# Four adaLN slabs moved to layer 0's routing with the first gather held free, and a ninth place for layer 1's expert slabs

## What is computed

```python
sh1, sc1, g1, sh2, sc2, g2 = jnp.split(silu(c) @ w_ada[l] + b_ada[l], 6, axis=-1)   # and the same for c_ctx
h = modulate(rms_norm(x, norm1_g[l]), sh1, sc1)          # latent and context tokens
y = parallel_mixer(h, ...)     # neighbourhood attention and HGRN2 branches, sigmoid gates, w_out
x = x + g1 * y
h2 = modulate(rms_norm(x, norm2_g[l]), sh2, sc2)
x = x + g2 * grouped_moe(h2, w_router, ...)              # 16 experts, top 2 of the best group of 4
```

## Time and profile before

| what | us |
|---|---|
| median of 3 runs | 1500.55 |
| lowest and highest | 1500.09, 1509.64 |
| the profiled execution | 1510.84 |
| its span, first to last instruction | 1508.8 |
| mean granted TensorE clock in it | 0.968 of 2.4 GHz |

### The profile page before, as it was taken

How to read it: one execution, slowest core, us unless ns; L and a number is a source line. 1 busy time by engine, 2 the same in 40 slices (tenths; PEclk the granted TensorE clock), 3 DMA queues, 4 the chain that set the end, 5 groups by cost and what they waited for, 6 DMA issues and landing times.

```text
span 1508.8 us, 17997 instructions
## 1 busy us (share of the span) xinstructions
PE 1408.4 (93%) x7084; PEld 973.6 (65%) x7084; DVE 903.3 (60%) x1234; ACT 687.6 (46%) x962; POOL 202.3 (13%) x179
## 2 busy tenths in 40 slices
PE   3999999998999985999999969989998998999997
PEld 2786667645888854677777638876766996334333
DVE  3477986456744436988888824688586874222112
ACT  4553452246333345777777626543346453111002
POOL 0006970000000001211111020058000000000000
PEclk9999999999999987999999977999999998999999
DMA  9861104693131435999999975111444664999994
GB/s 356 238 175 58 38 19 168 246 388 147 56 112 57 182 112 199 366 388 401 401 400 400 345 272 213 56 57 56 167 157 179 258 245 168 381 429 428 426 428 165
DMA packets 96764, 352.19 MB, mean 233 GB/s; under 512 B 21792, under 2 KB 22944, under 8 KB 84128
## 3 DMA queue, kind: packets, MB, share of 16 engines
q1 hardware_dynamic: 93008, 337.95, 58.6%
q0 software_dynamic: 2976, 10.49, 2.1%
q10 hardware_dynamic: 688, 2.49, 0.4%
HBM read 341.48 MB, written 13.63 MB: 235 GB/s over the span
## 4 chain that ended last, share of the span: by engine, by line
PE 81%; DVE 6%; POOL 4%; ACT 3%; DMA 2%; issue 2%; another core or an unknown queue 1%; ACTq 0%; SPq 0%; DVEq 0%; POOLq 0%
PE bank L1412 7%; PE bank L832 4%; PE bank L1147 4%; PE bank L1144 4%; PE bank L1153 4%; PE bank L1434 4%; PE bank L724 3%; PE bank L970 3%; PE bank L972 3%; PE bank L975 3%; PE bank L743 3%; PE bank L680 2%; PE bank L1173 2%; PE bank L1178 2%; PE bank L1183 2%; PE bank L1445 2%
## 5 line engine op out<-in xcount | busy, mean ns | idle before, releaser
L2985 DVE TENSOR_TENSOR slab_lo<-slab,high 128x4096 fp32r<-128x4096 f32 x48 | 210.8, 4417 | 4.7 <-ACT high L2114 4.7
L2114 ACT ACTIVATE high<-slab 128x4096 fp32r<-128x4096 f32 x48 | 174.1, 3631 | 21.5 <-PE bank L1153 19.8
L2390 POOL DMA_INDIRECT feed_rows<-token_table,slot_token x16 | 45.1, 2820 | 549.8 <-DVE slot_token L2926 359.6
L1412 PE MATMUL bank<-narrow_slab,picked 128*64 128x512 f32 x256 | 113.2, 595 | 2.1 <-issue 1.7
L1413 PE MATMUL bank<-narrow_slab,picked 128*64 128x512 f32 x256 | 113.3, 595 | 0.0
L832 PE MATMUL bank<-hT,ring 128*128 128x512 f32 (+1 forms) x256 | 104.2, 545 | 0.0
L3150 DVE TENSOR_TENSOR hidden<-bank,gated 64x512 f32<-64x512 f32 x16 | 17.4, 1085 | 134.6 <-ACT gated L2269 134.6
L1412 PEld LDWEIGHTS bank<-narrow_slab,picked 128*64 128x64 f32 x256 | 33.7, 137 | 66.6 <-issue 65.2
L832 PEld LDWEIGHTS bank<-hT,ring 128*128 128x128 f32 x256 | 46.8, 194 | 33.2 <-issue 31.6
L1144 PE MATMUL bank<-high,feed_hi 128*96 128x512 f32 x256 | 66.8, 404 | 0.7 <-ACT feed_hi L2121 0.7
L1147 PE MATMUL bank<-high,feed_lo 128*96 128x512 f32 x256 | 64.9, 395 | 1.6 <-DVE feed_lo L2992 1.6
(11 more groups left out here) (415 smaller groups left out, 3154.3 us busy)
## 6 DMA issues: line engine op xcount, KB each, us to landing
ring<-in_w_in SPq DMA_DIRECT2D x23, 2048.0 KB, 12.5
ring<-in_w_ada SPq DMA_DIRECT2D x20, 2048.0 KB, 10.5
slab<-in_w_gate SPq DMA_DIRECT2D x16, 2048.0 KB, 12.9
slab<-in_w_up SPq DMA_DIRECT2D x16, 2048.0 KB, 13.9
slab<-in_w_down SPq DMA_DIRECT2D x16, 2048.0 KB, 14.4
narrow_slab<-in_w_gate SPq DMA_DIRECT2D x16, 2048.0 KB, 21.1
narrow_slab<-in_w_up SPq DMA_DIRECT2D x16, 2048.0 KB, 23.0
narrow_slab<-in_w_down SPq DMA_DIRECT2D x16, 2048.0 KB, 18.4
```

Source lines behind the costliest of these rows:

```text
L1412: T.matmul(bank[0][0:64, :], x, gate[:, k, :], start=(k == 0), stop=(k == KT - 1))
L2114: S.activation(half_of(e, kind)[:], w[:], ACT.Copy)\
L2985: V.tensor_tensor(low[:], w[:], half_of(e, kind)[:].bitcast(f32), ALU.subtract)\
```

## The change

Slabs 10 to 13 leave the attention of layer 0 and are done in the routing: slab 10 ahead of `place`, 11 behind it, 12 and 13 and the group's turn behind `slots`. The six slabs that stay beside the attention are at the even pairs 0 to 10. Slabs 10 and 13 are fetched into the slabs of up and down of expert 1, slabs 11 and 12 into the place of `high[0]` and `high[1]`. So the splits of expert 0 on ACT wait for slabs 11 and 12 to be done, and the fetches of up and down of expert 1 wait for slabs 10 and 13, and up also for the first gathered rows. DVE now starts its first split only when POOL has gone past its first gather (`slots_kept` at 2). In layer 1 a ninth place is at the address of `xT`; it is first filled when x has been copied into PSUM.

```diff
-    ADA_GROUPS = ((0, 2), (1, 3), (4, 5), (6, 7, 8, 9), (10, 11, 12, 13), (14, 15), ...
+    ADA_GROUPS = ((0, 2), (1, 3), (4, 5), (6, 7, 8, 9), (14, 15), (10, 11, 12, 13), ...
...
-    FIRST, AGAIN = (6, 7, 0, 1, 2, 3, 4, 5), tuple(range(LANES))
+    FIRST, AGAIN = (6, 7, 0, 1, 2, 3, 4, 5, 8), tuple(range(LANES))
...
-    narrow_at = slab_at[:SLOTS] + [B0, hT_at, A0 + 16 * KB, B0 + 16 * KB]
+    narrow_at = slab_at[:SLOTS] + [B0, hT_at, A0 + 16 * KB, B0 + 16 * KB, xT_at]
...
+    gap_slab = [fixed(f"gap_slab{i}", [P, SLOT], offset=A0 + (44 + 16 * i) * KB) for i in range(2)]
...
+        GAP_LANES = (6, 7, 6, 7)
...
-            loads += ada_loads[4:16] if l == 0 else ada_loads[20:24]
-            turn += [1, 2, 3, 1, 2, 0, 3, 1, 2, 0, 3, 1] if l == 0 else [1, 2, 3, 1]
+            loads += ada_loads[4:10] + ada_loads[14:16] if l == 0 else ada_loads[20:24]
+            turn += [1, 2, 3, 1, 2, 0, 3, 1] if l == 0 else [1, 2, 3, 1]
...
+            if l == 0:
+                loads += ada_loads[10:14]
+                lane += GAP_LANES
...
+        def ada_place(n):
+            gap = {10: slab[LANE[UP][1]], 11: gap_slab[0], 12: gap_slab[1], 13: slab[LANE[DOWN][1]]}
+            return front_slab[n][:] if n < len(front_slab) else gap[n][:] if n in gap else slot(ada_loads[n])
...
-                return 6 + p if 0 <= p < 10 else None
+                return {0: 6, 2: 7, 4: 8, 6: 9, 8: 14, 10: 15}.get(p)
...
# tensor engine, routing
+                if l == 0:
+                    ada_rows(10)
                 o = open_bank(("place", l), "place_ready")
...
                 if l == 1:
                     x_as_rows(0)
+                else:
+                    ada_rows(11)
...
                     mm.then_inc(sem["psum_ready"], 1)
+                    ada_rows(12)
+                    ada_rows(13)
+                    ada_turn(13)
...
# SP, the first slabs of layer 0's experts
+                    def fill_gap(n):
+                        there, count = full(ada_loads[n])
+                        if n >= 12:
+                            sp.wait_ge(there, count - 16)
+                        sp.dma_start(ada_place(n).rearrange("p (k n) -> p k n", k=KT), source(ada_loads[n])[0]).then_inc(there, 16)
...
+                        if (e, kind) == (1, UP):
+                            sp.wait_ge(*slot_spent[max(m for m in range(base) if lane[m] == i)])
+                            fill_gap(10)
+                            sp.wait_ge(*is_ready(("out", 0, KT - 1)))
+                            fill_gap(11)
+                            fill_gap(12)
+                            sp.wait_ge(sem["h_ready"], 2 * KT)
+                            fill_gap(13)
+                            sp.wait_ge(*slot_spent[slot_of(ada_loads[10])])
+                            sp.wait_ge(sem["rows_there0"], 16)
+                            fill_slab(e, kind)
+                            continue
+                        if (e, kind) == (1, DOWN):
+                            sp.wait_ge(*slot_spent[slot_of(ada_loads[13])])
+                            fill_slab(e, kind)
+                            continue
...
# SP, layer 1's experts
+                        elif at == FIRST[-1]:
+                            sp.wait_ge(sem["h_ready"], KT * 4)
+                            sp.wait_ge(*is_ready(("x_rows", 0)))
...
# scalar engine
+                    act.wait_ge(*slot_spent[slot_of(ada_loads[11])])
                     split_high(0, GATE)
+                    act.wait_ge(*slot_spent[slot_of(ada_loads[12])])
                     split_high(0, UP)
+                    ada_keep(13)
                     keep_feed(0)
...
# gpsimd, in the loop of gathers
+                    if e == 0:
+                        pool.sem_inc(sem["slots_kept"], 1)
...
# vector engine
+                    dve.wait_ge(sem["slots_kept"], 2)
                     split_low(0, GATE)
+                    ada_mod(13)
                     keep_feed(0)
                     split_low(0, UP)
+                    dve.wait_ge(sem["ada_mod"], ada_group(13)[0] + 1)
```

More of the change, by code:

```diff
@@ L82, in fixed @@
         return nc.alloc_sbuf_tensor_at(name, shape, dtype, offset=where)
+    xT_at = at[0]
     xT = fixed("xT", [P, KT, TOK])
@@ L94, in build @@
     router = fixed("router", [P, KT, 32])
-    ADA_GROUPS = ((0, 2), (1, 3), (4, 5), (6, 7, 8, 9), (10, 11, 12, 13), (14, 15), (16, 17, 18, 19), (20, 21, 22, 23))
+    ADA_GROUPS = ((0, 2), (1, 3), (4, 5), (6, 7, 8, 9), (14, 15), (10, 11, 12, 13), (16, 17, 18, 19), (20, 21, 22, 23))
     COND_AT = 6
@@ L376, in loads_before @@
             counts = [lane[:b].count(i) for i in range(len(FIRST))]
-            assert len(set(counts[:SLOTS])) == 1
+            assert ph == 3 or len(set(counts[:SLOTS])) == 1
             return counts
@@ L402, in result @@
             return bank[ready[key][0]]
+        skews = 4 * NA_HEADS * DEPTH
         scatter_bank = (1, 5, 6, 7, 1, 5, 6, 7)
@@ L666, in ada_rows @@
                 pe.wait_ge(*full(ada_loads[n]))
-                w = (front_slab[n][:] if n < len(front_slab) else slot(ada_loads[n])).rearrange("p (k n) -> p k n", k=KT)
+                w = ada_place(n).rearrange("p (k n) -> p k n", k=KT)
                 if first:
@@ L1057, in x_as_rows @@
                         for j in range(4):
-                            T.matmul(bank[b][:, j * P:(j + 1) * P], xT[:, 4 * half + j, SEG + t * P:SEG + (t + 1) * P],
-                                     ident, start=(j == 0), stop=False)
+                            mm = T.matmul(bank[b][:, j * P:(j + 1) * P], xT[:, 4 * half + j, SEG + t * P:SEG + (t + 1) * P],
+                                          ident, start=(j == 0), stop=False)
+                    jobs[0] += 1
+                    ready["x_rows", half] = (None, jobs[0], "psum_ready")
+                    mm.then_inc(sem["psum_ready"], 1)
                 if l == 1:
@@ L1596, in _ @@
                         sp.wait_ge(sem[f"tok_there{t}"], 32)
-                while n < base:
+                gap_loads = slot_of(ada_loads[10]) if l == 0 else base
+                while n < gap_loads:
                     if last_in(n) not in slot_spent:
@@ L1602, in _ @@
                         sp.wait_ge(*is_ready(("o", l, HG_HEADS - 1)))
[L1603 removed]
+                        sp.wait_ge(sem["bias_loaded"], 16 * (skews + l))
                         sp.dma_start(bias_skew[:].rearrange("p h q c -> p (h q c)"), skew_table[l]).then_inc(sem["bias_loaded"], 16)
@@ L1620, in _ @@
                     n += 1
-                if n < base or ("place", l) not in ready:
+                if n < gap_loads or ("place", l) not in ready:
                     break
@@ L2702, in window_bias @@
                     if h == 0:
-                        dve.wait_ge(sem["bias_loaded"], 16 * (l + 1))
+                        dve.wait_ge(sem["bias_loaded"], 16 * (skews + l + 1))
                     b = bias[:, h].rearrange("p q (r c) -> p (q r) c", c=GRID_W)
@@ L2845, in _ @@
                 wide_gates()
-                dve.wait_ge(sem["ada_mod"], ada_group(12 * l + 11)[0] + 1)
+                dve.wait_ge(sem["ada_mod"], ada_group(12 * l + (9, 11)[l])[0] + 1)
                 for d in range(KT * l):
```

5 lines of the change are left out of this document (2 added, 3 removed).

## The result

The changed kernel takes 1496.93 us (median of 20 runs, 1493.52 to 1502.56); the kernel before takes 1508.2 us (median of 20 runs, 1500.09 to 1511.44). The ratio is 0.9937 with an interval of 0.9926 to 0.9947: 0.63% faster, inside 1%. I had forecast 0.87% and 1487.5 us. Of the 9.4 us between 1487.5 and 1496.93 most is the base: the median of three runs from which I started, 1500.55, lay at the low end of what 20 runs show.

A forecast was written before the change was run, and what follows sets the result against it. PE, busy 93% of the span, was taken as the bound. Gains of 9.9 (attention), 1.5 (routing) and 1.75 us (ninth place) sum to 13.15, scaled to a median of 1487.5 us; range 1480 to 1498.

The forecast's parts named there:

- Part 1: Layer 0's attention: 11.9 us of slabs, turn and slab waits saved, less 2.0 of new DVE-chain waits: 9.9 us gained.
- some 1.8 us either way: Layer 0's attention: allowance for one half-clock stretch more or less as PE's stalls change.
- Part 2: Layer 0's routing: four slabs and a turn fit into PE's idle time and rows turn earlier: 1.5 us gained.
- DVE now stays off until POOL is past it: Routing, first gather: free of DVE's split it takes 0.92 us, so its rows could be turned 3.4 us earlier.
- fourth rival: Routing: POOL lets DVE go before the gather's descriptors are written; routing gains 0, 11.65 us in all, 1489.0; chance 0.14 or 0.07.
- Both share the DMA engines with the stores of the token rows: Routing: fetches of slabs 12 and 13 run beside the token stores at a DMA share of 0.52, cost 0.
- The third limit: Routing: ACT's late splits, adaLN row copy, turn and DVE's addition let `turn_rows` start at 584.0, not 585.65: 1.6 gained.
- Part 3: Layer 1's experts: slabs issued a place earlier remove PE's wait at expert 15: 1.75 us gained.
- the first: Rival, layer 0's attention: DVE's chain takes the slabs' place, only 4.5 us gained there; 1492.8 us in all; chance 0.13.
- The second: Rival, routing: the gap runs at half clock, a loss of 1.7 us there; 1490.7 us in all; chance 0.12.
- The third: Rival, routing: clock stays up, so `turn_rows` and expert 0's first eight matmuls save 2.1 us more; 1485.4; chance 0.14.
- The fifth: Rival, layer 0's experts: bound by fetches, pushed work costs about 15.6 us against 13.15 gained; 1503 us; chance 0.04.

The follow-up runs named there:

- run 5: The changed kernel itself measured once more, nothing altered: 1500.28 us, ratio 0.9949 to the kernel before.
- run 6: Changed kernel with adaLN slab 13's fetch cut to an eighth, its products reading slab 10's place: 1494.09 us, ratio 0.9908.
- run 7: Changed kernel without DVE's wait for `slots_kept` ahead of its first split: 1497.44 us, ratio 0.9936.
- run 12: The changed kernel itself measured a third time, nothing altered: 1502.42 us.
- run 3: Changed kernel with DVE doing its adaLN addition first, then waiting for the first gathered rows to land before its split: 1495.71 us, ratio 0.9921.
- run 2: Changed kernel with eight places for layer 1's slabs again in place of nine: 1499.27 us, ratio 0.9944.
- run 1: Changed kernel with slabs 10 to 13 left out wholly, with their fetches and waits, and without DVE's wait for `slots_kept`: 1496.95 us, ratio 0.9926.
- run 4: Changed kernel with the six attention slabs beside pairs 1, 2, 3, 7, 9 and 11 in place of the even pairs: 1488.03 us, ratio 0.9865.

## Why the prediction was right or wrong

**Part 1, the attention (9.9 us).** The mechanism was right. The waits came where the chain was drawn: 0.60 at pair 0 (I had said 0.5), 1.77 at pair 2 (1.7), 0.98 at pairs 6 and 10 (0.7); the 2.41 at pair 14 was there before, as 2.40. That is 2.5 us of new waits where I had 2.0, and no wait for a slab is left. In the profile the gain is 12.5, because the clock went from 0.95 to 1.00. With one stretch at half clock, as in runs 5, 6 and 7, it is 11.1; with three, as in run 12, it is 8.1. The attention before had two such stretches, one behind each of its two waits for the scaling (windows, the number ahead of the last two is the clock):

```profile
343.00:353.00 10.00, 8.46 (x50) 5.16 (x52) 7.64 (x23) 6.64 (x20) 0.00 (x0) 0.83 1.03 393
355.00:365.00 10.00, 6.82 (x42) 4.42 (x40) 4.40 (x13) 5.90 (x12) 0.00 (x0) 0.83 0.00 0
```

By the changed kernel's 59.5, 60.9 and 63.9 us with none, one and three, a stretch costs some 1.4 us; with two of them, as before, the gain would be 9.6 us by this estimate, and 9.9 was forecast. The term "some 1.8 us either way" for the clock was the mis-sized one: 59.5 to 63.9 us is what the same program shows. This is also part of why profile (16.3 us) and medians (11.3 us) differ: the profile of before was of one of its slowest executions (1510.84, the runs reach 1511.44), the one after of one of its fastest (1494.57, the runs begin at 1493.52).

**Part 2, the routing (1.5 us gained).** This is the step that failed. In the profile after it lost 1.5 us up to the first turn and 0.8 us more to the second (10.0 us from the first turn to the second, where it was 9.2), as more of expert 0's first products fell into half clock: 3.70 and 2.62 us for the first two groups of eight, before 3.40 and 2.03. Two sentences of it were wrong.

"DVE now stays off until POOL is past it, so it takes 0.92 and not 4.33 us": POOL's signal stands behind the gather in its program but comes ahead of its work: DVE had begun at 564.69, the gather at 564.88. That was my fourth rival, to which I gave 0.07. The first profile shows the gather caught in spite of the hold, and run 5 the same program with a gather that went through: the outcome is left to a race. Run 3 shows what a real hold would have been worth: 3.2 us of span. The rival had priced itself at no gain, and the measured loss of 1.5 is more: a caught gather ends 0.8 us behind the split, and the split now begins 7.3 us after `place` in place of 5.4, since ACT's split ahead of it waits for slab 11 (ACT begins at 560.62, 3.2 us after `place`; before it was 0.1 ahead of it).

"Both share the DMA engines with the stores of the token rows, but the share in 550 to 571 was 0.52. Cost 0": the window of that share ends at 571, where the last store is issued (570.55), and the stores land up to 576.3. It told nothing of what the stores meet. The window after, 539 to 557, in which all four are issued, is full:

```profile
539.00:557.00 18.00, 15.59 (x80) 6.98 (x78) 9.42 (x28) 14.18 (x28) 0.00 (x0) 0.81 1.05 389
```

The last store landed 8.9 us after its issue in place of 5.7, and the gather waits for it. Run 6 shows it by taking seven eighths of one fetch away. This error comes first: in the forecast the gather began 6.3 us after `place` (577.58) and the split 7.3 (578.6), so the gather would have gone through with no hold at all; in run 6 it began at 5.5 and did. It was the late stores that put it at 7.4, where only a hold that holds could have saved it.

The third limit, ACT's and DVE's chain behind the slabs, was right in kind and size: `place` to turn 12.4 us in run 3 and 13.3 in run 5 (its adaLN turn at half clock), against 14.4 before, 2.0 and 1.1 us gained where I had 1.6. The four slabs' own products took 1.9 us each and lay in idle time.

**Part 3, the ninth place (1.75 us).** Right: 2.0 us in the profile, 1.7 by run 2.

**The rivals.** Of the first (the chain through DVE takes the slabs' place) the 2.5 us of new waits are the true part, but the stage gained far more than 4.5. The second, a gap at half clock, came near in its number (a loss of 1.7, measured 1.5), not in its mechanism: the slabs ran at full clock. The third, the clock staying up through the gap, came in part, but not where it had its price: the clock was 1.00 from 557 to 570 us and 0.50 from 570 to 580, a stretch of 10 us at half clock where before it was 17 and in run 1, without the slabs, 20.5. The rows' turn and the first eight products of expert 0 still fell into it; those eight took 3.70 us, before 3.40.

```profile
575.45 3.70 PE L1165 MATMUL bank<-high,feed_hi 128*96 128x512 f32 x8 [0.67 <-ACT feed_hi L2168]
```

The rule named beside that rival, from the Trainium skill, "TensorE: Matmul & The Clock Gate", section "What's actually happening", is not contradicted: PE stood idle for 2.88 us up to 568.38, ahead of the fall of the clock at 570, and for 3.86 just ahead of the rows' turn. The fifth, slower by fetches, did not come either: PE is busy 263.4 of 265 us in layer 0's experts.

That the time fell into the range owes something to the range's width: the base alone was 7.65 us too low.

## What to carry to other kernels

Before work that fills idle time is taken off an engine, draw the chain that it covered and put what remains beside the pairs whose chain is longest; here that choice was worth as much again as the whole change (run 4: 0.7 to 0.8% of the time, the change 0.6). A signal that POOL gives behind an indirect DMA in its program does not say that the DMA's work is done; let the other engine's long operation wait for the DMA's data. Price a fetch by the DMA share in the very microseconds in which something on the path is stored, not by a mean around it.

## What the runs showed of the hardware that was not expected

**A gather caught by a split ends 0.8 us behind it, whatever its start.** DVE's split takes 4.42 us, and the gather ends 0.79 us behind that before (581.12, 581.91), 0.80 after (569.11, 569.91), 0.79 in run 1 and 0.79 for the second gather of run 5 (570.68, 571.47). So its length of 4.33, 5.03 or 4.02 us says only when it began. A gather that begins ahead of the split takes 0.92 (run 6: 566.00, under a split from 566.20 on). POOL's spans are rough by the profile's own word, but these agree to 0.01 us. The Trainium skill, "SBUF — State Buffer", section "Who interferes with whom", says that DVE and GpSimd share a port pair, and that whichever comes first locks the other out for the whole instruction. Our rows agree where the split comes first; where the gather does, the split of run 6 began inside it and took 4.43 us as ever. The same page says that an operation with two inputs from SBUF, such as this subtraction, contends with a GpSimd instruction that reads SBUF, and infers that it leaves descriptor writing free. This gather writes descriptors, and it takes its indices from SBUF; these rows show that it is held up, and not by which of the two.

**The same program differs by 4.4 us in one stage with the same waits.** The granted clock alone made 59.5 or 63.9 us of the attention. A single profile of such a stage is one draw; the clock in its windows tells which one.
